# Routing gates of a product-key expert layer: one 256-column fp32r product per token in place of an fp32 product, spread over the projection tile

## The chip, the cores and the metric

The kernel runs on one core of a Trainium2 chip. The core has five engines that run their own instruction streams and meet through semaphores: TensorE (PE, matrix products, with its weight loads shown apart as PEld), VectorE (DVE), ScalarE (ACT), GpSimd (POOL) and SyncE (SP, which issues the transfers here). The metric is the device time of one execution in microseconds (us); lower is better.

## The reference, cut to what matters

The program is one decoder layer over 576 tokens (512 of a prompt, 8 sequences of 8): a normalisation, an input projection, an RWKV-7 branch and a retention branch, their merge and an output projection, and then a layer of 128 x 128 = 16384 single-neuron experts of which each token uses 8 heads x 16. The part that matters here is the last one:

```python
q = (xb @ peer_wq).reshape(PEER_BLOCK, PEER_HEADS, 2, PEER_QDIM // 2)
s = jnp.einsum('bhpd,hpnd->bhpn', q, peer_keys).astype(F32)
sv, si = lax.top_k(s, PEER_TOPK)
cand = sv[:, :, 0, :, None] + sv[:, :, 1, None, :]
sc, flat = lax.top_k(cand.reshape(PEER_BLOCK, PEER_HEADS, PEER_TOPK * PEER_TOPK), PEER_TOPK)
i1 = jnp.take_along_axis(si[:, :, 0], flat // PEER_TOPK, axis=-1)
i2 = jnp.take_along_axis(si[:, :, 1], flat % PEER_TOPK, axis=-1)
e = i1 * N_KEYS + i2
gate = jax.nn.softmax(sc, axis=-1)
h = jax.nn.gelu(jnp.einsum('bhkd,bd->bhk', peer_u[e], xb).astype(F32), approximate=False)
return jnp.einsum('bhk,bhkd->bd', (gate * h).astype(xb.dtype), peer_v[e])
```

The kernel does not gather experts. It computes the hidden value of every expert for every token (all of `peer_u` against all tokens), and weighs it with a gate matrix that is zero wherever a token did not choose the expert.

## The kernel before

Everything stays in fp32 or in fp32r, a form of fp32 that TensorE reads in one pass at lower precision. A product that needs more precision is written as three fp32r products of high and low parts (high x high, high x low, low x high); the high part is a ScalarE copy into fp32r, the low part a VectorE subtraction (`low`, line 140).

**The stage around the change** is `gates_stage`. Its backbone is 128 tiles of the hidden projection, one for each 128 experts. A tile t is 96 matmuls (16 blocks c of the model width; for each, two halves of 288 tokens with three products), written out by `project3` (lines 125, 126, 129) into PSUM buffer t % 2. `segments` gives every engine the same order: 4 x 5 tiles with the `early` steps (the choice of experts for 5 groups of 128 tokens), 4 x 12 tiles with the `middle` steps (the gate matrices), then the rest. An argument `late=1` puts PE, ACT and SP one tile ahead of DVE's count.

The **steps of a tile**, engine by engine:

- PE waits for `lowered` (the low part of the tile's weights) and for `gelu` (the PSUM buffer is free), and runs the 96 matmuls; the last one signals `through` (the semaphore `ah_tile_done`).
- ACT waits for `through`, applies Gelu from PSUM into `hs` (line 1944), waits for the weights of tile t + 2 and casts them into their high part `uh` (line 1947).
- DVE waits for that cast and subtracts into `ul` (line 140), which releases `lowered`.
- SP stores `hs` (line 1887) and loads the next weights, 1 MB (line 1885).

The **middle steps** build, for each token, a 128 x 128 gate matrix: a product of two one-hot blocks summed over the token's 128 choices, where one side carries the gates. Twelve tokens are done per tile, in three groups g of four, so 48 tiles cover 576 tokens:

- DVE: waits for `gated` of the group's last use, writes both one-hot blocks `hot` of four tokens (line 2048).
- POOL: multiplies one of them with the gates into `rows` (line 1974) and signals `rowed`.
- PE: after the tile, and for each group, waits for `rowed` and for `moved` (its PSUM bank is free again), and multiplies `hot` by `rows`, four fp32 matmuls of 128 columns (line 1920), then signals `gated`. There are three PSUM banks, one per group, and ACT starts `moved` at 3, so a group waits only for the same group of the tile before.
- ACT: after Gelu and cast, waits for `gated` and copies the group from PSUM into `stage`, with a stride of 48 elements (line 1963), and signals `moved`.
- SP: after every fourth tile waits for all of `moved` and stores `stage`, 3 MB, to memory (line 1892). ACT's next copy but one round waits for that store.

Afterwards `experts_stage` multiplies the hidden values by the gates and by `peer_v`.

## Time and profile before

| what | us |
|---|---|
| median of 3 runs | 6522.78 (6519.88 to 6525.54) |
| the profiled execution | 6519.62 |
| its span | 6517.8 |
| tiles with middle steps, 48 of them, from about 3282 to about 4020 in the span | about 738 |
| mean granted TensorE clock | 0.979 |

How to read it: the profile shows the span of one execution, 1.8 us less than that execution's time. Each engine's busy time is the union of its instructions. A matmul's duration includes its way through the array, so a stream of them overlaps, and what one costs is the distance between starts. In 40 slices of 163 us PE stands at nine tenths or more in all but a handful, and the slices of the 48 middle tiles are among the fullest.

### The profile page before, as it was taken

The numbers are of one execution on the slowest core, as the hardware profiler recorded it, in microseconds if no ns is written. First come the engines' busy times: TensorE is split into PE (matmuls) and PEld (weight loads), VectorE is DVE, ScalarE is ACT, GpSimd is POOL, SyncE is SP. The second block draws the span as 40 slices with busy tenths as digits, with TensorE's granted clock in tenths as the row PEclk, the third lists the DMA queues.
The fourth block names the chain that finished last, engine by engine and source line by source line (L and its number), as shares of the span: only waits on it lengthen the run. The fifth ranks groups of instructions, "written<-read, shape, count | busy, mean of one in ns | idle before, by whom it ended". The sixth has DMA issues, their size and how long they took to land. (4 is left out here: it accounts for less than half of the span.)

```text
span 6517.8 us, 109245 instructions
## 1 busy us (share of the span) xinstructions
PE 6224.3 (95%) x46455; PEld 5740.2 (88%) x46455; DVE 2750.5 (42%) x4165; ACT 1586.5 (24%) x1919; POOL 324.1 (5%) x250
## 2 busy tenths in 40 slices
PE   7999989999999899698999999999989999999998
PEld 7787879999999899698999999999978888888886
DVE  4566543223222232256744443111145555555554
ACT  3333322222222221221233333111121122112211
POOL 1010000000000000000023232000000000000000
PEclk9999999999999999899999999999999999999999
DMA  2111022222133323122233433333344444444442
GB/s 92 42 39 53 34 75 94 102 88 100 68 136 119 121 101 115 49 72 105 101 130 127 149 138 134 106 107 107 107 129 127 127 123 125 128 127 122 126 128 98
DMA packets 352490, 679.34 MB, mean 104 GB/s; under 512 B 220800, under 2 KB 227968, under 8 KB 311296
## 3 DMA queue, kind: packets, MB, share of 16 engines
q1 hardware_dynamic: 345200, 656.85, 30.7%
q10 hardware_dynamic: 7056, 19.00, 0.7%
q8 instruction: 192, 3.15, 0.2%
q14 instruction: 42, 0.34, 0.0%
HBM read 562.40 MB, written 113.37 MB: 104 GB/s over the span
## 5 line engine op out<-in xcount | busy, mean ns | idle before, releaser
L125 PE MATMUL ps<-hn_high,ah_uh 128*128 128x288 f32 x4096 | 1147.8, 296 | 23.2 <-DVE ah_ul L140 23.1
L126 PE MATMUL ps<-hn_low,ah_uh 128*128 128x288 f32 x4096 | 1140.5, 294 | 0.0
L2159 PE MATMUL ps<-va_vh,va_h_parts 128*128 128x512 f32 x2560 | 1007.2, 393 | 23.8 <-DVE va_h_parts L140 23.8
L2163 PE MATMUL ps<-va_vl,va_h_parts 128*128 128x512 f32 x2560 | 1015.4, 397 | 0.0
L129 PE MATMUL ps<-hn_high,ah_ul 128*128 128x288 f32 x4096 | 880.7, 296 | 0.0
L2161 PE MATMUL ps<-va_vh,va_h_parts 128*128 128x512 f32 x2048 | 814.4, 398 | 0.0
L125 PEld LDWEIGHTS ps<-hn_high,ah_uh 128*128 128x128 f32 x4096 | 771.1, 188 | 24.5 <-DVE ah_ul L140 23.4
L126 PEld LDWEIGHTS ps<-hn_low,ah_uh 128*128 128x128 f32 x4096 | 769.1, 188 | 0.0
L2231 DVE TENSOR_TENSOR va_y<-va_y,ps 128x512 f32<-128x512 f32 x640 | 440.5, 688 | 772.8 <-PE ps L2163 772.8
L140 DVE TENSOR_TENSOR ah_ul<-ah_u,ah_uh 128x2048 fp32r<-128x2048 f32 x128 | 293.5, 2293 | 1085.4 <-ACT ah_uh L1947 1077.2
L129 PEld LDWEIGHTS ps<-hn_high,ah_ul 128*128 128x128 f32 x4096 | 655.5, 188 | 0.0
L2159 PEld LDWEIGHTS ps<-va_vh,va_h_parts 128*128 128x128 f32 x2560 | 483.9, 189 | 137.3 <-issue 24.0
L2163 PEld LDWEIGHTS ps<-va_vl,va_h_parts 128*128 128x128 f32 x2560 | 482.2, 188 | 114.1
L1094 PE MATMUL ps<-rwkv_hn_high,ret_wh 128*128 128x288 f32 x1664 | 494.5, 312 | 16.1 <-DVE ret_wl L140 16.1
L1095 PE MATMUL ps<-hn_low,ret_wh 128*128 128x288 f32 x1664 | 472.1, 298 | 0.0
L2161 PEld LDWEIGHTS ps<-va_vh,va_h_parts 128*128 128x128 f32 x2048 | 383.7, 187 | 95.2
L2182 ACT CAST va_vh<-va_v 128x1024 fp32r<-128x1024 f32 x256 | 255.5, 1045 | 520.0 <-PE ps L2163 512.0
L1944 ACT ACTIVATE ah_h<-ps 128x576 f32<-128x576 f32 x128 | 83.4, 652 | 1226.4 <-PE ps L129 1226.4
L1098 PE MATMUL ps<-rwkv_hn_high,ret_wl 128*128 128x288 f32 x1664 | 358.1, 297 | 0.0
L1094 PEld LDWEIGHTS ps<-rwkv_hn_high,ret_wh 128*128 128x128 f32 x1664 | 320.4, 193 | 28.9 <-DVE ret_wl L140 16.2
L609 PE MATMUL ps<-rwkv_hn_high,rwkv_wh 128*128 128x288 f32 (+1 forms) x960 | 297.1, 324 | 27.2 <-DVE hn_low L140 27.2
L1095 PEld LDWEIGHTS ps<-hn_low,ret_wh 128*128 128x128 f32 x1664 | 319.6, 192 | 2.1
(376 smaller groups left out, 10174.9 us busy)
## 6 DMA issues: line engine op xcount, KB each, us to landing
ah_u<-peer_u SPq DMA_DIRECT2D x128, 1024.0 KB, 5.0
va_v<-peer_v SPq DMA_DIRECT2D x256, 512.0 KB, 3.6
ret_w<-w_ret SPq DMA_DIRECT2D x48, 1024.0 KB, 4.9
h_kept<-ah_h SPq DMA_DIRECT2D x128, 288.0 KB, 2.1
gates<-ah_stage SPq DMA_DIRECT2D x12, 3072.0 KB, 9.7
va_h<-h_kept SPq DMA_DIRECT2D x128, 288.0 KB, 3.1
va_g<-gates SPq DMA_DIRECT2D x128, 288.0 KB, 3.9
rwkv_w<-w_rkv SPq DMA_DIRECT2D x24, 1024.0 KB, 4.8
```

What stands on the lines that cost most here:

```text
L125: pe.matmul(out[:, h, :], wh[:, c, :], ah[:, c, t], start=(c == 0), stop=False)
L126: pe.matmul(out[:, h, :], wh[:, c, :], al[:, c, t], start=False, stop=False)
L129: last = pe.matmul(out[:, h, :], wl[:, c, :], ah[:, c, t], start=False, stop=(c == k - 1))
L140: return dve.tensor_tensor(out, whole, high.bitcast(F32), ALU.subtract)
L609: pe.matmul(z[:, h, :], w, K.hn_high[:, c, t], start=(c == 0), stop=False)
L1094: pe.matmul(z[:, h, :], w, K.high[:, c, t], start=(c == 0), stop=False)
L1095: pe.matmul(z[:, h, :], w, K.low[:, c, t], start=False, stop=False)
L1098: last = pe.matmul(z[:, h, :], v, K.high[:, c, t], start=False, stop=(c == DC - 1))
L2159: done = pe.matmul(Z[bank], mine, high, start=(j == 0), stop=False)
L2161: pe.matmul(Z[bank], hx[:, s, j, 2 * T - TP + P * m:2 * T - TP + P * m + P], high, start=False, stop=False)
L2163: done = pe.matmul(Z[bank], mine, lows, start=False, stop=(j == R - 1))
L2231: dve.tensor_tensor(part, part, Z[bank], ALU.add).then_inc(added, 1)
```

## The change

Each gate matrix is computed in fp32r. `slots[:, 2]` (the gates) is split into `gate_h`, an fp32r copy that ACT makes beside its copy into `slots`, and `gate_l`, a DVE subtraction made once. POOL now makes two products per group, with the high and with the low part, side by side in `rows` (twice its former size). PE makes one matmul of 256 columns per token in place of one fp32 matmul of 128. A group now fills two PSUM banks (high halves and low halves beside each other), so four banks make two buffers, and group g of tile k uses buffer (k + g) % 2; `moved` starts at 2.

On leaving PSUM the halves are added: ACT copies the high half into `stage` and signals `half` (the semaphore `ah_high_half_staged`), and DVE adds the low half from PSUM onto it in `stage` and signals `moved`. After each add DVE writes the one-hot block for the same group one tile ahead; the first three are written before the middle tiles (`ahead`), which also takes them out of the wait for `gated`.

PE's groups no longer stand behind the tile: they follow blocks c = 4, 9 and 15 of the 16. The tile's matmuls are written out in `tile` for that (lines 1916, 1917, 1920 after the change).

The norm stage only allocates fewer semaphores (three lines, not shown).

```diff
@@ -1829,10 +1829,11 @@
             return nc.alloc_sbuf_tensor_at("ah_" + name, shape, dt, offset=place), place + 4 * int(np.prod(shape[1:]))
 
         stage, room = over("stage", [P, ROWS, TC], room)
-        hot, room = over("hot", [P, 2, TURN, P], room)
-        rows, room = over("rows", [P, TURN, P], room)
+        hot, room = over("hot", [P, 2, TURN, P], room, F32R)
+        rows, room = over("rows", [P, TURN, 2, P], room, F32R)
         sb("rest", [P, (room - nc.sbuf_base) // 4])
         iota = sb("iota", [P, P])
+        gate_h, gate_l = sb("gate_high", [P, NTT * P], F32R), sb("gate_low", [P, NTT * P])
         u, base = over("u", [P, 2, DC, P], K.x1_at)
         ul, base = over("ul", [P, 2, DC, P], base, F32R)
         assert base <= K.x1_at + 4 * DC * T
@@ -1845,12 +1846,16 @@
         consts = sem("consts")
         diff, exped, ided, turned, slotted = sem("diff"), sem("exp"), sem("ids"), sem("turned"), sem("slots")
         hotted, rowed, gated, moved = sem("hot"), sem("rows"), sem("gates"), sem("staged")
+        parted, half = sem("gate_parts"), sem("high_half_staged")
         stored = sem("stage_stored")
         Z = [K.ps[:, 2 * n:2 * n + 2, 0:HT] for n in range(2)]
-        X = [K.ps[:, 4 + n, :] for n in range(3)]
+        X = [K.ps[:, 4 + 2 * n:6 + 2 * n, :].rearrange("p b (t x i) -> p b t x i", t=2, x=2) for n in range(2)]
         block = ctx.enter_context(nc.Block())
 
-        def segments(eng, tile, early, middle, late=1):
+        def staged(k, g):
+            return stage[:, :, 12 * k + 4 * g:12 * k + 4 * g + 4].rearrange("p i (b t) -> p b t i", b=2)
+
+        def segments(eng, tile, early, middle, late=1, between=None):
 
             if late:
                 tile(0, 0, True)
@@ -1858,10 +1863,15 @@
                 for k in range(4):
                     tile(4 * i + k + late, (k + late) % 2, True)
                     early(i, k)
+            if between:
+                between()
             with eng.Fori(0, NST) as s:
                 for k in range(4):
-                    tile(EARLY + 4 * s + k + late, (k + late) % 2, True)
-                    middle(s, k)
+                    if eng is nc.tensor:
+                        tile(EARLY + 4 * s + k + late, (k + late) % 2, True, lambda g: middle(s, k, g))
+                    else:
+                        tile(EARLY + 4 * s + k + late, (k + late) % 2, True)
+                        middle(s, k)
             n = (ROWS - 2 - MIDDLE - late) // 2
             with eng.Fori(0, n) as i:
                 for k in range(2):
@@ -1888,7 +1898,7 @@
 
             def middle(s, k):
                 if k == 3:
-                    sp.wait_ge(moved, 12 * s + 15)
+                    sp.wait_ge(moved, 12 * s + 14)
                     sp.dma_start(K.gates[:, s, :, :], stage[:, :, :]).then_inc(stored, 16)
             segments(sp, tile, nothing, middle)
             for s in range(2):
@@ -1897,10 +1907,21 @@
 
         @block.tensor
         def _(pe):
-            def tile(t, s, more):
+            def tile(t, s, more, group=None):
                 pe.wait_ge(lowered, t + 1)
                 pe.wait_ge(gelu, t + 1)
-                project3(pe, Z[s], uh[:, s, :, :], ul[:, s, :, :], K.hh, K.hl).then_inc(through, 1)
+                for c in range(DC):
+                    for h in range(2):
+                        m = slice(h * HT, h * HT + HT)
+                        pe.matmul(Z[s][:, h, :], uh[:, s, c, :], K.hh[:, c, m], start=(c == 0), stop=False)
+                        pe.matmul(Z[s][:, h, :], uh[:, s, c, :], K.hl[:, c, m], start=False, stop=False)
+                    for h in range(2):
+                        m = slice(h * HT, h * HT + HT)
+                        last = pe.matmul(Z[s][:, h, :], ul[:, s, c, :], K.hh[:, c, m], start=False, stop=(c == DC - 1))
+                    if c == DC - 1:
+                        last.then_inc(through, 1)
+                    if group and c in (4, 9, 15):
+                        group((4, 9, 15).index(c))
 
             def early(i, k):
                 if k == 3:
@@ -1911,15 +1932,15 @@
                                             K.ident[:, :])
                     last.then_inc(turned, 1)
 
-            def middle(s, k):
-                for g in range(3):
-                    n = 12 * s + 3 * k + g
-                    pe.wait_ge(rowed, n + 1)
-                    pe.wait_ge(moved, n + 1)
-                    for t in range(4):
-                        last = pe.matmul(X[g][:, P * t:P * t + P], hot[:, 1, 4 * g + t, :], rows[:, 4 * g + t, :],
-                                         start=True, stop=True)
-                    last.then_inc(gated, 1)
+            def middle(s, k, g):
+                n = 12 * s + 3 * k + g
+                pe.wait_ge(rowed, n + 1)
+                pe.wait_ge(moved, n + 1)
+                for t in range(4):
+                    last = pe.matmul(K.ps[:, 4 + 2 * ((k + g) % 2) + t // 2, 2 * P * (t % 2):2 * P * (t % 2) + 2 * P],
+                                     hot[:, 1, 4 * g + t, :], rows[:, 4 * g + t, :, :].rearrange("p x i -> p (x i)"),
+                                     start=True, stop=True)
+                last.then_inc(gated, 1)
             pe.sem_inc(gated, 3)
             segments(pe, tile, early, middle)
 
@@ -1927,7 +1948,7 @@
         def _(act):
             act.sem_inc(gelu, 2)
             act.sem_inc(slotted, 1)
-            act.sem_inc(moved, 3)
+            act.sem_inc(moved, 2)
             act.sem_inc(stored, 16)
             for s in range(2):
                 act.sem_inc(kept[s], 16)
@@ -1952,6 +1973,7 @@
                     act.activation(ids[:, 2, :, :], ids[:, 2, :, :], ACT.Exp).then_inc(exped, 1)
                 if k == 3:
                     act.wait_ge(turned, i + 1)
+                    act.copy(gate_h[:, bass.ds(P * i, P)], K.ps[:, 7, 2 * P:3 * P])
                     act.copy(slots[:, :, bass.ds(P * i, P)], K.ps[:, 7, 0:3 * P].rearrange("p (s t) -> p s t", s=3))\
                         .then_inc(slotted, 1)
 
@@ -1960,19 +1982,21 @@
                     act.wait_ge(stored, 16 * s + 16)
                 for g in range(3):
                     act.wait_ge(gated, 12 * s + 3 * k + g + 4)
-                    act.copy(stage[:, :, 12 * k + 4 * g:12 * k + 4 * g + 4].rearrange("p i t -> p t i"),
-                             X[g].rearrange("p (t i) -> p t i", t=4)).then_inc(moved, 1)
+                    act.copy(staged(k, g), X[(k + g) % 2][:, :, :, 0, :]).then_inc(half, 1)
             segments(act, tile, early, middle)
 
         @block.gpsimd
         def _(pool):
+            pool.wait_ge(parted, 1)
             with pool.Fori(0, NST) as s:
                 for k in range(4):
                     for g in range(3):
                         t = slice(4 * g, 4 * g + 4)
                         pool.wait_ge(hotted, 12 * s + 3 * k + g + 1)
-                        pool.tensor_tensor(rows[:, t, :], hot[:, 0, t, :],
-                                           slots[:, 2, bass.ds(TC * s + 12 * k + 4 * g, 4)]
+                        own = bass.ds(TC * s + 12 * k + 4 * g, 4)
+                        pool.tensor_tensor(rows[:, t, 0, :], hot[:, 0, t, :].bitcast(F32), gate_h[:, own].bitcast(F32)
+                                           .unsqueeze(2).broadcast_to([P, 4, P]), ALU.mult)
+                        pool.tensor_tensor(rows[:, t, 1, :], hot[:, 0, t, :].bitcast(F32), gate_l[:, own]
                                            .unsqueeze(2).broadcast_to([P, 4, P]), ALU.mult).then_inc(rowed, 1)
 
         @block.vector
@@ -2039,16 +2063,24 @@
                         .then_inc(ided, 1)
                     dve.drain()
 
+            def one_hot(g, first):
+                dve.tensor_tensor(hot[:, :, 4 * g:4 * g + 4, :],
+                                  iota[:, :].unsqueeze(1).unsqueeze(1).broadcast_to([P, 2, 4, P]),
+                                  slots[:, 0:2, bass.ds(first, 4)].unsqueeze(3).broadcast_to([P, 2, 4, P]), ALU.is_equal)\
+                    .then_inc(hotted, 1)
+
+            def ahead():
+                dve.wait_ge(slotted, NTT + 1)
+                dve.tensor_tensor(gate_l[:, :], slots[:, 2, :], gate_h[:, :].bitcast(F32), ALU.subtract).then_inc(parted, 1)
+                for g in range(3):
+                    one_hot(g, 4 * g)
+
             def middle(s, k):
-                if k == 0:
-                    dve.wait_ge(slotted, NTT + 1)
                 for g in range(3):
-                    t = slice(4 * g, 4 * g + 4)
-                    dve.wait_ge(gated, 12 * s + 3 * k + g + 1)
-                    dve.tensor_tensor(hot[:, :, t, :], iota[:, :].unsqueeze(1).unsqueeze(1).broadcast_to([P, 2, 4, P]),
-                                      slots[:, 0:2, bass.ds(TC * s + 12 * k + 4 * g, 4)].unsqueeze(3)
-                                      .broadcast_to([P, 2, 4, P]), ALU.is_equal).then_inc(hotted, 1)
-            segments(dve, tile, early, middle, 0)
+                    dve.wait_ge(half, 12 * s + 3 * k + g + 1)
+                    dve.tensor_tensor(staged(k, g), staged(k, g), X[(k + g) % 2][:, :, :, 1, :], ALU.add).then_inc(moved, 1)
+                    one_hot(g, TC * s + 12 * k + 4 * g + 12)
+            segments(dve, tile, early, middle, 0, ahead)
 
 
 def experts_stage(nc, K, a, x1):
```

**PE, from the end of a middle tile to the start of the next one, before.** The names are those of the program; `ps` is PSUM, and a row's waits stand in brackets.

```order
L129 MATMUL ps<-hn_high,ah_ul 128x288 x2
L1917 ISA
L1920 MATMUL ps<-ah_rows,ah_hot 128x128 [waits ah_staged,ah_rows]
L1920 MATMUL ps<-ah_rows,ah_hot 128x128 x3
L1917 REGISTER_ALU
L1920 MATMUL ps<-ah_rows,ah_hot 128x128 [waits ah_staged,ah_rows]
L1920 MATMUL ps<-ah_rows,ah_hot 128x128 x3
L1917 REGISTER_ALU
L1920 MATMUL ps<-ah_rows,ah_hot 128x128 [waits ah_staged,ah_rows]
L1920 MATMUL ps<-ah_rows,ah_hot 128x128 x3
L1901 REGISTER_ALU
L125 MATMUL ps<-hn_high,ah_uh 128x288 [waits ah_gelu_done,ah_u_low]
```

The same place after the change; the first row is among the last three matmuls of block c = 15.

```order
L1917 MATMUL ps<-hn_low,ah_uh 128x288
L1920 MATMUL ps<-hn_high,ah_ul 128x288 x2
L1937 REGISTER_ALU
L1940 MATMUL ps<-ah_rows,ah_hot 128x256 [waits ah_staged,ah_rows]
L1940 MATMUL ps<-ah_rows,ah_hot 128x256 x3
L1911 REGISTER_ALU
L1916 MATMUL ps<-hn_high,ah_uh 128x288 [waits ah_gelu_done,ah_u_low]
```

Three groups of 128 columns have become one group, the third, of 256 columns behind the tile's last matmul, which signals `ah_tile_done`; the other two stand inside the tile, each with the same two waits.

**ACT, one middle tile from its wait for the end of the tile to the first group's copy, before.**

```order
L1943 ISA [waits ah_tile_done]
L1944 ACTIVATE ah_h<-ps 128x576 [waits ah_h_stored0]
L1946 REGISTER_ALU
L1947 CAST ah_uh<-ah_u 128x2048 [waits ah_u_in0]
L1962 REGISTER_ALU
L1963 COPY ah_stage<-ps 128x4x128 [waits ah_gates]
L1962 REGISTER_ALU
```

And after:

```order
L1964 ISA [waits ah_tile_done]
L1965 ACTIVATE ah_h<-ps 128x576 [waits ah_h_stored0]
L1967 REGISTER_ALU
L1968 CAST ah_uh<-ah_u 128x2048 [waits ah_u_in0]
L1984 REGISTER_ALU
L1985 COPY ah_stage<-ps 128x4x128 [waits ah_gates]
L1984 REGISTER_ALU
```

Nothing moved here: the three copies follow the wait for the tile's end, the Gelu and the cast.

**DVE, one middle tile, before** (the low part of the weights, then the one-hot blocks):

```order
L1987 REGISTER_ALU
L140 TENSOR_TENSOR ah_ul<-ah_u,ah_uh 128x2048 [waits ah_u_high]
L2047 REGISTER_ALU
L2048 ISA [waits ah_gates]
L2048 TENSOR_TENSOR ah_hot<-ah_iota,slots 128x2x512
L2047 REGISTER_ALU
L2048 ISA [waits ah_gates]
```

And after:

```order
L140 TENSOR_TENSOR ah_ul<-ah_u,ah_uh 128x2048 [waits ah_u_high]
L2080 ISA
L2081 TENSOR_TENSOR ah_stage<-ah_stage,ps 128x4x128 [waits ah_high_half_staged]
L2067 ISA
L2067 TENSOR_TENSOR ah_hot<-ah_iota,slots 128x2x512
L2080 REGISTER_ALU
L2081 TENSOR_TENSOR ah_stage<-ah_stage,ps 128x4x128 [waits ah_high_half_staged]
L2067 ISA
L2067 TENSOR_TENSOR ah_hot<-ah_iota,slots 128x2x512
L2080 REGISTER_ALU
```

An add that waits for ACT's copy now stands before each one-hot block, and the block is the next tile's.

## Rows read from the trace of the kernel before

**Rows 1.** The page: busy time of each engine, share of the span, instructions.

```profile
PE 6224.3 (95%) x46455; PEld 5740.2 (88%) x46455; DVE 2750.5 (42%) x4165; ACT 1586.5 (24%) x1919; POOL 324.1 (5%) x250
```

**Rows 2.** Busy time by window: early tiles, and middle tiles; first row names columns.

```profile
core 0: us, PE busy (x) PEld busy (x) DVE busy (x) ACT busy (x) POOL busy (x), PEclk, DMA share, GB/s
3080.00:3285.00 205.00, 204.23 (x1535) 202.46 (x1534) 164.49 (x328) 51.46 (x47) 0.00 (x0) 1.00 0.30 103
3290.00:4026.00 736.00, 736.00 (x5746) 736.00 (x5745) 311.65 (x190) 260.77 (x240) 230.83 (x144) 1.00 0.37 134
```

**Rows 3.** PE in order of time: start, duration, instruction, count. Two gate bursts.

```profile
3310.30 2.84 PE L1920 MATMUL ps<-ah_rows,ah_hot 128*128 128x128 f32 x24
3312.90 0.38 PE L125 MATMUL ps<-hn_high,ah_uh 128*128 128x288 f32 x1
...
3325.68 2.84 PE L1920 MATMUL ps<-ah_rows,ah_hot 128*128 128x128 f32 x24
```

**Rows 4.** PE by window: 288-column matmuls only, then 512-column ones (window, length, busy, clock).

```profile
4100.00:4600.00 500.00, 500.00 (x3784) 1.00 0.30 107
5400.00:6300.00 900.00, 900.00 (x3865) 1.00 0.45 126
```

**Rows 5.** PE, then ACT, in order of time around one tile's end; idle before in brackets.

```profile
3617.83 2.84 PE L1920 MATMUL ps<-ah_rows,ah_hot 128*128 128x128 f32 x24
...
3605.12 1.91 ACT L1947 CAST ah_uh<-ah_u 128x2048 fp32r<-128x2048 f32 x1 [1.72 <-DMA ah_u<-peer_u]
...
3618.12 0.65 ACT L1944 ACTIVATE ah_h<-ps 128x576 f32<-128x576 f32 x1 [8.12 <-PE ps L129]
3618.66 1.89 ACT L1947 CAST ah_uh<-ah_u 128x2048 fp32r<-128x2048 f32 x1
3620.45 3.07 ACT L1963 COPY ah_stage<-ps 128x512 f32<-128x512 f32 x3
```

**Rows 6.** Instructions of single lines: durations in ns, minimum, median, maximum.

```profile
L1963 ACT COPY ah_stage<-ps x144: 1102/1197/1238, 3297.6 to 4022.1; 128x512 f32<-128x512 f32 x144
...
L2231 DVE TENSOR_TENSOR va_y<-va_y,ps x640: 686/689/690, 4798.7 to 6466.0; 128x512 f32<-128x512 f32 x160
...
L894 DVE TENSOR_REDUCE rwkv_kk<-rwkv_cs x16: 1059/1064/1085, 211.9 to 918.4; 128x64 f32<-128x512 f32 x16
```

**Rows 7.** PE by window after idle time: first and last of nine, and one between.

```profile
946.97:956.97 10.00, 10.00 (x58) 10.00 (x59) 2.29 (x1) 0.16 (x1) 0.00 (x0) 0.75 0.77 316
...
2677.17:2681.51 4.34, 0.00 (x1) 0.00 (x0) 0.76 (x1) 0.73 (x2) 0.00 (x0) 0.72 0.04 4
2681.51:2691.51 10.00, 9.99 (x32) 7.57 (x33) 0.00 (x0) 9.83 (x16) 0.00 (x0) 0.78 0.01 2
...
6480.44:6490.44 10.00, 10.00 (x34) 7.62 (x35) 0.00 (x0) 9.82 (x16) 0.00 (x0) 0.83 0.00 0
```

**Rows 8.** PE's waits (total, times, longest); then windows behind two such waits.

```profile
PE ps L657 <- DVE rwkv_ksq L805: 17.9, 7, 2.6
...
339.83:346.83 7.00, 6.69 (x34) 6.26 (x34) 6.40 (x10) 1.92 (x2) 0.00 (x0) 0.76 0.26 101
...
239.40:246.40 7.00, 5.15 (x34) 4.71 (x34) 6.40 (x10) 1.91 (x2) 0.00 (x0) 1.00 0.27 110
```

**Rows 9.** VectorE and GpSimd instructions of the middle steps, durations in ns as in group 6.

```profile
L2048 DVE TENSOR_TENSOR ah_hot<-ah_iota,slots x144: 1215/1221/2066, 3287.5 to 4009.4; 128x1024 f32<-128x1024 f32 x144
...
L1974 POOL TENSOR_TENSOR ah_rows<-ah_hot,slots x144: 1033/1857/2021, 3288.9 to 4012.3; 128x512 f32<-128x512 f32 x144
```

**Rows 10.** VectorE in order of time, one middle tile: weights' low part, one-hot blocks.

```profile
3620.59 2.29 DVE L140 TENSOR_TENSOR ah_ul<-ah_u,ah_uh 128x2048 fp32r<-128x2048 f32 x1 [6.99 <-ACT ah_uh L1947]
3622.80 4.33 DVE L2048 TENSOR_TENSOR ah_hot<-ah_iota,slots 128x1024 f32<-128x1024 f32 x3
```

**Rows 11.** SyncE's queue: the store of the stage and the next load of weights.

```profile
3592.93 0.33 SPq L1892 DMA_DIRECT2D gates<-ah_stage  x1
3593.80 0.35 SPq L1885 DMA_DIRECT2D ah_u<-peer_u  x1
```

**Rows 12.** ScalarE's copies into the slots, durations in ns, first and last start.

```profile
L1955 ACT COPY slots<-ps x5: 473/482/483, 3078.2 to 3285.2; 128x384 f32 x5
```

More of the change, by code:

```diff
@@ L146, in norm_stage @@
     with ExitStack() as ctx:
-        ld = [ctx.enter_context(nc.semaphore(tag + f"_loaded{q}")) for q in range(4)]
+        ld = [ctx.enter_context(nc.semaphore(tag + f"_loaded{q}")) for q in range(4)] if load is not None else []
         sq = ctx.enter_context(nc.semaphore(tag + "_squared"))
@@ L152, in norm_stage @@
         dn = ctx.enter_context(nc.semaphore(tag + "_normed"))
-        st = ctx.enter_context(nc.semaphore(tag + "_stored"))
-        hi = ctx.enter_context(nc.semaphore(tag + "_high"))
+        st = ctx.enter_context(nc.semaphore(tag + "_stored")) if store is not None else None
+        hi = ctx.enter_context(nc.semaphore(tag + "_high")) if parts else None
         rstd = ctx.enter_context(nc.sbuf_tensor(tag + "_r", [P, T], F32))
```

## The prediction

> **What bounds the kernel now.** I read the page first: TensorE is busy 95% of the span [rows 1]. That is an average, so I went to the windows of the gates stage. In the 736 us that hold nearly all the middle tiles PE is busy for all 736 us at full granted clock; DVE is busy 312 us, ACT 261, POOL 231 [rows 2]. So here every microsecond of PE work counts in full, and everything else has more than half its time free. Then PE in order of time, for what one middle tile consists of. From one gate burst to the next it is 3325.68 - 3310.30 = 15.38 us. The burst, 24 records for 12 tokens, holds PE from 3310.30 to 3312.90, which is 2.60 us [rows 3]. A plain 288-column matmul costs 500 / 3784 = 0.132 us [rows 4], so 96 of them are 12.68 us, and the burst's whole price is 15.38 - 12.68 = 2.70 us.
>
> **What the change removes.** The 24 records (two per fp32 product) become 12 matmuls of 256 columns. Rows show 0.132 us for 288 columns and 900 / 3865 = 0.233 us for 512 [rows 4]; on the line through both, 256 columns cost 0.118 us, 12 of them 1.41 us. So PE's own work falls by 2.70 - 1.41 = 1.29 us per tile, 62 us over 48 tiles. If the clock and the waits stay as they are, that is the whole effect.
>
> The page "FP8 and Floating Point Precision" of the Trainium skill (TensorE Precision Notes) has true fp32 take four passes through the array, which would put the new product at half of the old one's columns, 1.35 us per tile and a saving of 65 us. The trace shows two records per product, not four, and I keep the line through its two rows.
>
> **What the change adds: a wait behind the tile.** Follow the third group, g = 2. It uses the same PSUM buffer as g = 0 of the same tile, (k + g) % 2. `moved` starts at 2, and group n waits for n + 1, so it needs n - 1 groups moved, the last of which is g = 0 of its own tile. That group was multiplied early, after block 4. But who moves it? ACT's copy stands in ACT's queue behind the wait for the end of the same tile, the Gelu and the cast; the order of ACT's instructions is unchanged. So PE finishes its 96 matmuls, arrives at g = 2 and stands still until ACT has worked down to g = 0 and DVE has added the low half. Before, with three banks, a group waited for the group of the tile before, long done.
>
> The length of this stand, from the moment PE would issue g = 2:
>
> 1. to the Gelu's start: 3618.12 - 3617.83 = 0.29 us [rows 5].
> 2. Gelu to the start of the cast 0.54 us, cast to the start of the first copy 1.79 us [rows 5].
> 3. the first copy to its end: 1.10 us, the lowest of its line, since the first of three is the shortest [rows 6]. Sum so far 3.72 us. The copy of the high half has the same 512 elements and the same stride of 48, so I keep its price.
> 4. DVE's add, 512 elements from PSUM and strided `stage` back to `stage`. No row shows it. The same add without a stride takes 0.69 us (L2231); a reduction that reads 512 elements with a stride of 64 takes 1.06 us (L894) [rows 6]. ACT's strided copy takes 1.20 us. I take 1.06, the nearest in kind, with bounds of 0.69 and 1.5 (both read and write strided). DVE is idle at this time.
> 5. two hand-overs between engines, about 0.1 us together.
>
> That is 3.72 + 1.06 + 0.1 = 4.9 us per tile, in full on PE, since PE's queue is in order and the next tile's first matmul stands behind g = 2. The period becomes 12.68 + 1.41 + 4.9 = 19.0 us against 15.38: +3.6 us per tile, 48 tiles, +174 us.
>
> **The clock.** PE never stands still in the middle tiles now; then it would for nearly 5 us in each. In the trace of before there are, past its first 100 us, nine stands of 3 us or more, and behind each the granted clock is at its lower level, 1.2 GHz, for part of the next 10 us: the mean of the nine is 0.77, from 0.72 to 0.83, the stand of 4.34 us has 0.78 [rows 7]. Behind stands of 2.3 to 2.6 us it is mixed: 0.76 in one 7 us window, 1.00 in another [rows 8]. So 4.9 us should always cost clock. A mean of 0.78 over 10 us is 2.2 us of full-speed work lost; bounds 1.7 and 2.8. I take 2.2 us per tile, +106 us. Nothing hides it, since PE is the chain. The period is then 21.2 us.
>
> **Smaller parts.**
>
> - First middle tile: the first one-hot blocks wait for `slots`. ACT's last copy starts at 3285.2 [rows 12] and gets a small copy ahead of it (0.2 us); DVE's subtraction of 640 elements (0.75 us by L140's 2.29 us for 2048) and a one-hot block of 1.22 us follow, then two POOL products of 1.0 to 2.0 us. `rowed` comes at about 3290 to 3292, while PE is at block 4 at about 3286. One stand of some 5 us with 2 us of clock: +7 us, once.
> - POOL: two products where there was one. Alone one takes 1.03 us, beside DVE's one-hot block up to 2.02 [rows 9]. Six are 6.2 to 12.1 us in a period of 21 us. For the next tile's g = 0: its one-hot block starts when the add ends at 4.9, ends at 6.1, and two products are done at 8.2, or 9.4 if DVE's next block goes between. PE wants them five blocks after g = 2, at 4.9 + 0.5 + 4.0 = 9.4 us, and 2 us later at the low clock. No wait.
> - DVE: weights' low part 2.29, three blocks 4.33 [rows 10], three adds 3.2, together 9.8 us; the low part is late in the period, at about 15 us, but it is wanted one tile later. Hidden. The subtraction of the whole `gate_l` is in the first part.
> - SP: the store waits for the last add, about 9.4 us behind the tile's end in place of 5.9, and the load of weights behind it (3593.80 after 3592.93 [rows 11]) is as late. Today the cast behind such a store waits 1.72 us for that load [rows 5], and PE doesn't notice. With a period of 21.2 us, 5.8 longer, the 3.5 us of delay are covered: 0. With a period of 19.0 they are nearly not: up to 1.7 us for each of 11 stores.
>
> **Sum.** Period: 21.2 - 15.38 = 5.8 us x 48 = 280 us, plus 7 = 287 us. On the profiled execution's 6519.6 us that gives 6807; the median of the runs is 3.2 us higher, so 6810 us. The gain of 62 us is in this sum; it is paid back four times over.
>
> **Rivals.**
>
> - *The clock stays up.* For it: one 2.58 us stand left it at 1.00 [rows 8], and PE is dense around the stand. Against: all nine stands over 3 us lowered it. Then 48 x 3.6 + 5 + 11 x 1.7 = 197 us: 6720 us; with the cheap add of 0.69 us 6700.
> - *More waits than the one.* If the add costs 1.5 us and POOL's products reach g = 0 about 1 us late, each tile is 1.4 us longer: 6877. Rows 9 show that a one-hot block of 1.22 us becomes 2.06 us beside POOL, and POOL's product doubles. The Trainium skill, "SBUF — State Buffer" (Who interferes with whom), calls this an exclusive lock: a DVE instruction with two SBUF inputs and a GpSimd one that reads SBUF take turns whole. By it POOL's two products wait for at most one block between them, the 9.4 us above. The add reads one operand from PSUM and would be free of it.
> - *Faster.* The mechanism is the shorter burst alone: g = 2 finds its buffer free, because group 0 is moved before the tile ends. It decides at one point, the place of ACT's first copy: it would have to be ahead of ACT's wait for the tile's end. Then -62 us and +7: 6519.6 - 55 + 3.2 = 6468. Against it stands the order of ACT's instructions, where it is behind. Only a misreading of the semaphore's count could save this case.
> - *No change*, where a short stand of about 1.2 us without clock loss cancels the gain: 6523. No row gives such a length.
>
> **Chances.** Forecast 0.75 (its own range, from the bounds of add and clock: 6765 to 6860), clock stays up 0.10, more waits 0.08, faster 0.05, same 0.02. The range of 6700 to 6890 takes in the first three. A difference under 0.2%, 13 us, couldn't be told from no change here; by that, faster 0.05, same 0.02, slower 0.93.
>
> **What the profile of the changed kernel would show.** In the middle tiles, PE no longer busy throughout: about 4.9 us idle in each of 48 tiles, ended by DVE's add into `ah_stage`; Gelu starts 19 to 21 us apart; 12 products per tile at 0.118 us where the clock is full; a granted clock of about 0.8 to 0.9 as the mean of the stretch. The add between 0.7 and 1.5 us. The tiles before and after the middle unchanged at 12.7 us, and the stages around them too. What would make it wrong: idle time of PE ended by POOL's `rows` in every tile (the second rival), a clock of 1.00 (the first), or no idle time before g = 2 (the third).

## The result, and the profile after

| | us |
|---|---|
| before, median (4 runs) | 6521.77 (6519.88 to 6525.54) |
| changed, median (4 runs) | 6782.63 (6780.55 to 6786.51) |
| changed / before | 1.040, 95% interval 1.039 to 1.041 |
| profiled execution, before and changed | 6519.62 and 6780.63 |
| 48 tiles, from the Gelu of the first middle tile to the Gelu behind the last one, before and changed | 738.1 and 991.0 |

The change costs 4%. The page's first lines, as in rows 1:

```profile
PE 6251.6 (92%) x45879; PEld 5758.1 (85%) x45879; DVE 2944.9 (43%) x4313; ACT 1581.6 (23%) x1924; POOL 574.4 (8%) x394
```

DVE and POOL have 194 and 250 us more to do, PE much the same over a longer span. The windows of the gates stage answer to rows 2: the early tiles, the middle tiles, and plain tiles behind them (columns as there).

```profile
3080.00:3285.00 205.00, 204.20 (x1535) 202.46 (x1534) 164.56 (x328) 51.84 (x50) 0.00 (x0) 1.00 0.29 103
3290.00:4276.00 986.00, 761.32 (x5150) 751.48 (x5150) 498.04 (x331) 250.11 (x236) 480.24 (x287) 0.90 0.27 99
4330.00:4770.00 440.00, 440.00 (x3329) 440.00 (x3329) 80.24 (x35) 85.45 (x70) 0.00 (x0) 1.00 0.31 106
```

Before and behind the middle tiles nothing moved: early tiles have the same busy time to 0.1 us on PE. In the middle tiles PE, which was busy all the time, is idle for 225 of 986 us, at a granted clock of 0.90. I call such idle time of PE before an instruction a stand. The list of waits in the stage says who ends it (who waits, for whom, total, times, longest; not all rows are shown):

```profile
PEld ps L1940 <- issue: 237.0, 48, 5.3
PE ps L1940 <- DVE ah_stage L2081: 227.1, 48, 5.1
ACT ah_stage L1985 <- PE ps L1940: 76.2, 48, 1.7
...
PEld ps L1940 <- POOL ah_rows L1999: 5.8, 1, 5.8
PE ps L1940 <- POOL ah_rows L1999: 5.6, 1, 5.6
```

48 waits, one in each middle tile, 4.73 us on average, all before a gate product and all ended by DVE's add. One more, 5.6 us, is the first tile's. Here is one of the 48 in order of time, PE, ACT and DVE (start, duration, instruction, idle time before it); it answers to rows 5.

```profile
3613.03 0.43 PE L1920 MATMUL ps<-hn_high,ah_ul 128*128 128x288 f32 x2
3618.23 1.19 PE L1940 MATMUL ps<-ah_rows,ah_hot 128*128 128x256 f32 x4 [4.78 <-DVE ah_stage L2081]
...
3613.57 0.65 ACT L1965 ACTIVATE ah_h<-ps 128x576 f32<-128x576 f32 x1 [13.60 <-PE ps L1920]
3614.12 1.89 ACT L1968 CAST ah_uh<-ah_u 128x2048 fp32r<-128x2048 f32 x1
3615.91 1.87 ACT L1985 COPY ah_stage<-ps 128x512 f32<-128x512 f32 x2
3619.46 1.06 ACT L1985 COPY ah_stage<-ps 128x512 f32<-128x512 f32 x1 [1.68 <-PE ps L1940]
...
3616.95 1.13 DVE L2081 TENSOR_TENSOR ah_stage<-ah_stage,ps 128x512 f32<-128x512 f32 x1 [10.01 <-ACT ah_stage L1985]
```

Read from top to bottom in time it is the chain of the prediction: the tile's last matmuls at 3613.03, Gelu at 3613.57, cast, the copy of group 0 at 3615.91, the add at 3616.95, and 0.15 us after the add's end PE goes on with group 2 at 3618.23. Its four products take 1.19 us with their way through the array, at the lower clock; four such products take 0.64 us at full clock elsewhere in the tile.

Durations of single lines in ns, minimum, median and maximum: the new product, and the add.

```profile
L1940 PE MATMUL ps<-ah_rows,ah_hot x576: 277/283/583, 3292.0 to 4281.2; 128*128 128x256 f32 x192
...
L2081 DVE TENSOR_TENSOR ah_stage<-ah_stage,ps x144: 1008/1127/1261, 3307.7 to 4283.4; 128x512 f32<-128x512 f32 x144
```

The median distance between two of these products' starts is 0.118 us at full clock.

### The profile page after: what moved, and what is told of

The parts are those of the page before. It is cut to its first block and busy times, and to the rows that moved or that the text cites. A ratio compares the mean times of both kernels' runs of the same rounds, so it can differ in the third digit from the quotient of the medians.

```text
span 6778.9 us, 108539 instructions
## 1 busy us (share of the span) xinstructions
PE 6251.6 (92%) x45879; PEld 5758.1 (85%) x45879; DVE 2944.9 (43%) x4313; ACT 1581.6 (23%) x1924; POOL 574.4 (8%) x394
## 5 line engine op out<-in xcount | busy, mean ns | idle before, releaser
L1916 PE MATMUL ps<-hn_high,ah_uh 128*128 128x288 f32 x4096 | 1178.3, 302 | 23.0 <-DVE ah_ul L140 22.9
L1917 PE MATMUL ps<-hn_low,ah_uh 128*128 128x288 f32 x4096 | 1172.1, 300 | 0.0
L1920 PE MATMUL ps<-hn_high,ah_ul 128*128 128x288 f32 x4096 | 896.4, 301 | 0.0
L1916 PEld LDWEIGHTS ps<-hn_high,ah_uh 128*128 128x128 f32 x4096 | 802.0, 196 | 24.3 <-DVE ah_ul L140 23.1
L1917 PEld LDWEIGHTS ps<-hn_low,ah_uh 128*128 128x128 f32 x4096 | 798.8, 195 | 0.0
L1920 PEld LDWEIGHTS ps<-hn_high,ah_ul 128*128 128x128 f32 x4096 | 673.7, 193 | 0.0
L140 DVE TENSOR_TENSOR ah_ul<-ah_u,ah_uh 128x2048 fp32r<-128x2048 f32 x128 | 333.5, 2606 | 657.3 <-ACT ah_uh L1968 649.3
L2081 DVE TENSOR_TENSOR ah_stage<-ah_stage,ps 128x512 f32<-128x512 f32 x144 | 161.6, 1122 | 491.2 <-ACT ah_stage L1985 491.2
L1997 POOL TENSOR_TENSOR ah_rows<-ah_hot,ah_gate_high 128x512 fp32r<-128x512 f32 x144 | 248.6, 1726 | 1062.3 <-DVE ah_hot L2067 1062.3
```

The lines of the kernel that those rows point to most:

```text
L140: return dve.tensor_tensor(out, whole, high.bitcast(F32), ALU.subtract)
L1916: pe.matmul(Z[s][:, h, :], uh[:, s, c, :], K.hh[:, c, m], start=(c == 0), stop=False)
L1917: pe.matmul(Z[s][:, h, :], uh[:, s, c, :], K.hl[:, c, m], start=False, stop=False)
L1920: last = pe.matmul(Z[s][:, h, :], ul[:, s, c, :], K.hh[:, c, m], start=False, stop=(c == DC - 1))
```

## Experiments: what makes PE stand

My theory (A) was that group 2 waits for a buffer that ACT can only empty after the end of the same tile. The rivals were that the stand has a length of its own (the add, the new products), and that spreading the groups over the tile costs by itself. All ratios are to the kernel before on the same chip. Each edit is shown in part; the label of the run stands in its heading, and the text calls it by its first part (e1, e2 and so on).

### Group 0 and 1 copied before the tile's end (`e1_early_copy`)

```diff
+                    elif eng is nc.scalar:
+                        middle(s, k, (0, 1))
+                        tile(EARLY + 4 * s + k + late, (k + late) % 2, True)
+                        middle(s, k, (2,))
```

The last argument names the groups that ACT copies there.

> The changed kernel, but ACT copies groups 0 and 1 of a tile before it waits for that tile's end; only group 2 is copied after Gelu and cast. Theory A (the stand before group 2 is ACT's queue order): three of four tiles take 12.68 + 1.41 = 14.1 us with no stand. The tile behind each store still stands: the copy of its group 0 waits until the stage is in memory (store issued about 5.5 us after the tile's end, 9.7 us to land, then 1.1 of copy and 1.1 of add: about 17.4 us, where PE wants group 2 at 14.1), 3 us of stand and up to 1.7 us of clock in 11 tiles. Time about 6520 - 62 + 8 + 11 x 4.5 = 6515 us (6480 to 6530). Rival B (the stand is the length of the add or the group products themselves, wherever the copy stands): 20.6 us per tile as in the changed kernel, 6780 us.

Measured: 6517.85 us, ratio 0.999 (0.998 to 1.000). The stands are gone in all but the tiles behind a store (PE's waits in this kernel's stage):

```profile
PE ps L1944 <- DVE ah_stage L2085: 30.4, 11, 2.8
```

and those come from ACT's copy waiting for the store of the stage:

```profile
ACT ah_stage L1989 <- DMA gates<-ah_stage: 122.1, 11, 11.1
```

Most rounds of four tiles take 14.1, 14.2, 16.2 and 16.6 us from Gelu to Gelu: ACT's late copy delays the Gelu behind it, so that one stand of 2.8 us and the clock behind it show in two of them. In nine of the eleven rounds the clock fell; in the other two the last of the four takes 15.1 us. Theory A holds: moving two copies in one queue, with the add, the products and the spread as they were, takes back 265 us. Of the gain of 62 us about 6 are left, at the edge of the noise, since a copy early in the tile meets a store that takes 9.6 us to land.

### The same, with the stage stored in two halves (`e2_early_copy_half_stage`)

```diff
-        stage, room = over("stage", [P, ROWS, TC], room)
+        stage, room = over("stage", [P, 2, ROWS, TC // 2], room)
...
-                if k == 3:
-                    sp.wait_ge(moved, 12 * s + 14)
-                    sp.dma_start(K.gates[:, s, :, :], stage[:, :, :]).then_inc(stored, 16)
+                if k % 2:
+                    sp.wait_ge(moved, 12 * s + 3 * k + 5)
+                    sp.dma_start(K.gates[:, 2 * s + k // 2, :, :], stage[:, k // 2, :, :]).then_inc(stored[k // 2], 16)
```

> As e1_early_copy, and the stage is stored in two halves of 24 tokens, each by its own transfer after every second tile, so no copy waits for a store (in memory the gates lie in runs of 96 bytes instead of 192, which the experts stage reads). Theory A: all middle tiles take 14.1 us but the first, clock 1.00, 6520 - 62 + 8 = 6466 us (6455 to 6480), faster than both kernels. Rival B: 6780 us. Rival C (shorter runs make the reads of the gates late in the experts stage): the middle tiles as in A, but the experts stage longer by some of its 128 reads, over 6480 us.

Measured: 6472.88 us, ratio 0.992 (0.990 to 0.994), faster than both kernels. A stretch of 600 us of its middle tiles has PE without a gap at full clock:

```profile
3300.00:3900.00 600.00, 600.00 (x4575) 600.00 (x4575) 464.86 (x296) 280.69 (x211) 339.29 (x255) 1.00 0.41 148
```

48 tiles take 678.4 us, 14.13 each, which is 59.7 us less than before. The first middle tile's stand costs 9.0 us of that again. The reads of the gates in the experts stage take a median of 4.5 us instead of 3.9, and that stage is no longer for it (1671.8 us against 1671.3 from its first to its last such matmul in the changed kernel): rival C falls.

### Two plain tiles ahead of the middle ones (`e7_two_plain_tiles`)

```diff
-    EARLY = 4 * NTT
+    EARLY = 4 * NTT + 2
...
+            for t in range(4 * NTT, EARLY):
+                tile(t + late, (t + late) % 2, True)
```

> e2_early_copy_half_stage with two plain tiles between the early and the middle ones, so that the split of the gates and the first one-hot blocks have a tile's time before PE wants them. Theory A (the rest of the loss is one stand of 5.8 us in the first middle tile and the clock behind it, 9.0 us from one Gelu to the next): 6473 - 9 = 6464 us (6458 to 6470). Rival G (PE's wait moves with the middle tiles, since a later step sets it): 6473 us.

Measured: 6470.06 us (6464.6 to 6471.3), ratio 0.992 (0.990 to 0.993). In the profile the first stand is gone and the stage is 8.3 us shorter than in e2, from its first Gelu to its last; the medians differ by 2.8 us, within the spread of either. The mechanism is shown, its worth in the time is not resolved.

### The spread alone, first attempt (`e5_spread_only`)

```diff
-                project3(pe, Z[s], uh[:, s, :, :], ul[:, s, :, :], K.hh, K.hl).then_inc(through, 1)
...
+                    if group and c in (4, 9, 15):
+                        group((4, 9, 15).index(c))
```

> The kernel before with one part of the change alone: its fp32 products of 128 columns, three single PSUM banks and ACT's copies stay, but the three groups follow blocks 4, 9 and 15 of the tile instead of standing behind it. Theory A (the spread does no harm by itself; the stand comes from two buffers for three groups): each group still waits only for the same group of the tile before, so no stand, 15.4 us per tile, time within 0.2% of the kernel before (6510 to 6535 us), a few us up for the first tile, whose group 0 waits for its one-hot block. Rival E (breaking up the tile costs: each of three entries and exits of a burst has its own gap): 0.1 to 0.2 us per entry, 5 to 20 us slower.

Measured: 6764.54 us, ratio 1.037 (1.036 to 1.039). My expectation was wrong, and so was that of rival E. PE's waits:

```profile
PE ps L1933 <- POOL ah_rows L1987: 149.9, 46, 4.5
```

PE stands 3.3 us before group 0, for POOL. In the kernel before, the one-hot blocks of a tile are written after the low part of the weights, at the beginning of the tile, and PE wanted them 12.7 us (96 x 0.132) after the tile's first matmul. Behind block 4 it wants them after 4.0 us (30 x 0.132). So this run said nothing about the spread itself; it showed that the spread needs the lookahead on DVE that the change also brings.

### The spread with its lookahead, and then two banks instead of three (`e9_spread_ahead`, `e10_two_banks`)

The first adds the change's `ahead` and one-hot blocks a tile early to e5; the second differs from it in the banks and the counts that go with them.

```diff
-                    last = pe.matmul(X[g][:, P * t:P * t + P], hot[:, 1, 4 * g + t, :], rows[:, 4 * g + t, :],
+                    last = pe.matmul(X[(k + g) % 2][:, P * t:P * t + P], hot[:, 1, 4 * g + t, :], rows[:, 4 * g + t, :],
...
-            act.sem_inc(moved, 3)
+            act.sem_inc(moved, 2)
```

> e5_spread_only (fp32 products, three single banks, groups behind blocks 4, 9 and 15) with the change's other half of the order: DVE writes the one-hot block of a group one tile ahead. In e5 PE stood 3.2 us before group 0, waiting for POOL's product of that tile's own one-hot block. Theory A (that wait is the missing lookahead, and with three banks nothing else stands): 15.4 us per tile, clock 1.00, 6522 + 9 for the first tile = 6531 us (6525 to 6545). Rival E (breaking the tile up costs by itself): over 6545 us, or PE idle inside the tiles.

> e9_spread_ahead with one thing changed: two PSUM banks instead of three, group g in bank (k + g) % 2, as in the changed kernel. No fp32r, no halves, no add. Theory A (the count of buffers with ACT's queue order is the whole cause): PE stands before group 2 from the tile's end to the end of ACT's first copy, 0.3 + 0.5 + 1.8 + 1.1 = 3.7 us, plus 1.6 us of clock: 20.7 us per tile, about 6785 us (6770 to 6800). Rival I (the add on DVE or the fp32r form is part of the cause): as e9, 6531 us.

Measured: 6538.60 us, ratio 1.002 (1.001 to 1.003), and 6789.26 us, ratio 1.041 (1.039 to 1.043). PE's waits, the first kernel's and then the second's:

```profile
PE ps L1935 <- ACT ah_stage L1978: 6.4, 11, 0.7
```

```profile
PE ps L1935 <- ACT ah_stage L1978: 161.8, 45, 3.6
```

With three banks the spread costs 14 us: 6 us in the first middle tile, and 0.8 us in every fourth, where ACT waits for the weights behind the store and is late with a bank. With two banks each tile takes 20.8 us, 3.6 of them a stand, here ended by ACT's copy since there is no add. This is the cleanest evidence for the cause: fp32 products of 128 columns, no halves, no add, and all of the loss, from a buffer count and a queue's order.

## Experiments: the price of the products

One run, `e6_one_pass_128`, on the kernel before:

```diff
-        hot, room = over("hot", [P, 2, TURN, P], room)
-        rows, room = over("rows", [P, TURN, P], room)
+        hot, room = over("hot", [P, 2, TURN, P], room, F32R)
+        rows, room = over("rows", [P, TURN, P], room, F32R)
```

> The kernel before with its twelve products per tile in fp32r and 128 columns, the high part alone (the low part of the gates is left out of the computation), groups behind the tile as before. Theory A (an fp32r product costs by its columns, on the line of 0.118 us for 256 and 0.132 for 288): 0.06 us each, 0.73 us per tile in place of 2.70, time 6522 - 48 x 1.97 = 6427 us. Rival F (a short product is bounded by its weight load, as the two passes of the fp32 one with 0.111 us per 128 columns may be): up to 0.11 us each, 1.3 us per tile, 6455 us; then the second 128 columns of the change cost next to nothing on PE.

Measured: 6457.82 us, ratio 0.990 (0.989 to 0.992). This kernel leaves out the low part of the gates. Its tiles take 14.04 us, and the median distance between two products is 0.111 us, within 0.001 us the distance between the two records of an fp32 product. So rival F has the price right: 128 columns in fp32r cost 0.111 us, as much as one of the two records in fp32, and 256 columns cost 0.118. The line through 288 and 512 columns was good down to 256 and fails at 128, where it gives 0.060. That the weight load sets this price was not shown. The low half of the change costs PE 0.007 us per token; almost all of its gain comes from one record in place of two.

## Experiments: the clock behind the stand

### The stand filled with work (`e3_filler`)

```diff
                     if c == DC - 1:
                         last.then_inc(through, 1)
+                        if group:
+                            pe.wait_ge(gelu, t + 2)
+                            for x in range(36):
+                                pe.matmul(K.ps[:, 2 * (1 - s):2 * (1 - s) + 2, 0:HT][:, x % 2, :], K.hh[:, c, 0:P],
+                                          K.hh[:, c, 0:HT], start=True, stop=True)
```

`pe.wait_ge(gelu, t + 2)` asks for the Gelu of the tile before, which is long done: the extra matmuls start at once.

> The changed kernel with 36 more 288-column matmuls per middle tile, between the tile's end and group 2, into the PSUM buffer that the next tile overwrites; they are no part of the result and take 36 x 0.132 = 4.75 us, the length of the stand. Theory A (4.7 us of stand, and 1.6 us per tile from the lower clock behind it): PE is never idle for more than 0.3 us, the clock stays at 1.00, the period falls from 20.65 to about 19.0 us although PE does more work, time 6780 - 48 x 1.6 = 6703 us (6690 to 6715). Rival D (the 1.6 us are waits inside the tile or slower group products, not clock): the period stays at 20.6 or grows, 6780 us or more.

Measured: 6736.09 us, ratio 1.032 (1.031 to 1.034). PE does 36 matmuls more per tile and the kernel is 47 us faster than the changed one: the clock was a part of the loss (first the changed kernel's stretch, then this one's, then who waits in it).

```profile
3300.00:3900.00 600.00, 462.56 (x3125) 456.63 (x3124) 304.87 (x203) 154.26 (x145) 291.38 (x174) 0.90 0.28 102
```

```profile
3300.00:3900.00 600.00, 586.21 (x4402) 579.68 (x4402) 317.82 (x211) 165.32 (x152) 305.58 (x184) 1.00 0.28 104
```

```profile
PE ps L1945 <- DVE ah_stage L2086: 19.4, 22, 1.7
ACT ah_uh L1973 <- DMA ah_u<-peer_u: 20.3, 12, 4.7
```

It is 33 us slower than I expected. Two parts of that show in its trace: ACT's cast waits 1.4 us for the weights behind each store (eleven times; the wait of 4.7 us comes behind the last middle tile), which is now on the chain (every fourth tile takes 20.6 to 20.8 us instead of 19.2 to 19.5), and copy and add are nearly 0.1 us longer each, so that group 2 starts 5.05 us behind the tile in the median instead of 4.86. In the eleven tiles behind a store 1.5 to 1.7 us of idle time are left, and the clock fell in none of them.

### The stand shortened (`e4_copy_before_gelu`)

```diff
             def tile(t, s, more, first=None):
                 act.wait_ge(through, t + 1)
+                if first:
+                    first()
                 act.wait_ge(kept[s], turns16(t, s))
```

where `first` is the copy of group 0.

> The changed kernel, but ACT copies group 0 right after the tile's end, before Gelu and cast. Theory A (the stand is a chain whose links add up): Gelu 0.54 and cast 1.79 us leave the chain, so the stand falls from 4.7 to about 2.4 us; clock as behind the 2.3 to 2.6 us stands of the kernel before, lost in some tiles only, 0 to 1.7 us per tile. Period 14.1 + 2.5 + 0 to 1.7 = 16.6 to 18.3 us, time 6590 to 6670 us. Rival B (the stand has a fixed length set by add or product): 6780 us.

Measured: 6625.77 us, ratio 1.015 (1.013 to 1.017). PE's waits:

```profile
PE ps L1943 <- DVE ah_stage L2086: 121.9, 48, 3.2
```

The stand is 2.5 us on average: Gelu and cast left the chain, and its links add up. Tiles take 16.8 us, which is 14.1 + 2.6, or 18.3, with 1.5 us of clock. Where group 0's copy waits for a store, the Gelu behind it is 0.8 us late (a tile of 17.6 us) and the stand is 3.0 to 3.2 us; four such stands took more of the clock (19.4 us). By these lengths the clock fell in 13 of 48 tiles: in 8 of the 38 with a stand of 2.4 or 2.5 us, and in 5 of the 10 with one of 3.0 to 3.2. The mean clock of the stretch is 0.96:

```profile
3300.00:3900.00 600.00, 512.92 (x3706) 505.33 (x3705) 334.70 (x238) 177.77 (x170) 310.99 (x206) 0.96 0.32 118
```

### Half of the filling, three quarters of it (`e8_half_filler`, `e11_filler_27`)

> The changed kernel with 18 extra matmuls behind the tile in place of e3_filler's 36 (no part of the result): the wait ends at the same time, but PE idles about 2.5 us of it. Theory A (the clock falls by how long PE idles, not by the wait): loss between none and the full 1.6 us per tile, as in e4_copy_before_gelu (18.3 us where the clock fell, 16.8 where not), period 19.3 to 20.2, time 6740 to 6775 us. Rival H (any wait of PE on VectorE costs the same clock): 20.65 us, 6780 us.

> The changed kernel with 27 extra matmuls behind the tile (no part of the result), so that PE idles about 1.2 us of the wait. With 36 the clock stayed at 1.00, with 18 (2.4 us idle) it fell in nearly every tile. If the clock needs a longer idle time than 1.2 us to fall: period 19.2 to 19.5, as with 36, 6736 us. If any idle time does it: 20.6, 6783 us.

Measured: with 18 matmuls 6783.56 us, ratio 1.040 (1.039 to 1.042); with 27, 6734.74 us, ratio 1.033 (1.031 to 1.035). PE's waits in the one with 18 and in the one with 27, then the stretch of each:

```profile
PE ps L1945 <- DVE ah_stage L2086: 106.8, 45, 2.7
```

```profile
PE ps L1945 <- DVE ah_stage L2086: 73.4, 47, 2.8
```

```profile
3300.00:3900.00 600.00, 530.97 (x3656) 524.91 (x3655) 303.99 (x203) 153.85 (x145) 290.59 (x176) 0.91 0.28 102
```

```profile
3300.00:3900.00 600.00, 552.46 (x4109) 545.47 (x4107) 316.28 (x211) 166.00 (x154) 301.45 (x180) 0.99 0.29 106
```

With 18 the stand is 2.4 us, half of the changed kernel's, and the whole price is paid, in 45 of 48 tiles by their length. That is over the range I gave: it is the time that rival H named, and what speaks against H is e3, e4 and e11. In e11 the mean of 1.6 us is made of two lengths: 37 stands of 1.1 to 1.3 us, none of which cost the clock, and 11 of 2.6 to 2.8 us behind the stores, of which three did. So short stands are free of it, and the price at 2.4 us did not fit e4, where stands of that length cost the clock in 8 of 38 tiles.

### The same idle time in a longer tile (`e12_longer_tile`)

```diff
+                    if group and c == 12:
+                        pe.wait_ge(gelu, t + 2)
+                        for x in range(17):
+                            pe.matmul(K.ps[:, 2 * (1 - s):2 * (1 - s) + 2, 0:HT][:, x % 2, :], K.hh[:, c, 0:P],
+                                      K.hh[:, c, 0:HT], start=True, stop=True)
```

added to e4, so that the stand is left alone and the tile gets longer.

> e4_copy_before_gelu with 17 extra matmuls after block 12 of each middle tile (no part of the result), far from the stand: the stand of 2.5 us stays, the period without clock loss becomes 16.8 + 2.2 = 19.0 us, that of e8_half_filler. Theory J (for the same idle time, the period decides how often the clock falls: e8 with 20.6 us lost it in nearly every tile, e4 with 16.8 in about every third): it falls in nearly every tile here, period about 20.5, 6522 + 48 x 5.1 + 9 = 6776 us. Rival K (what stands beside the idle time decides, not the period): as in e4, a mean loss of 0.7 us, period 19.7, 6738 us.

Measured: 6777.07 us, ratio 1.039 (1.037 to 1.041). Its stretch and PE's waits:

```profile
3300.00:3900.00 600.00, 525.48 (x3631) 519.55 (x3632) 288.66 (x207) 149.99 (x145) 268.98 (x178) 0.91 0.28 103
```

```profile
PE ps L1948 <- DVE ah_stage L2091: 108.7, 45, 2.5
```

All tiles but the first take 20.4 to 20.6 us. The stand is 2.4 us as in most tiles of e4, only the work between two stands is longer, and the clock goes from 0.96 to 0.91. So between these two kernels the distance between stands decides how often a stand of this length costs the clock. It is not the whole rule: in e1, stands of 2.7 to 2.8 us come some 60 us apart and cost it in nine of eleven cases; in e11, stands of 2.6 to 2.8 us with short ones between them did in three of eleven. The five kernels with idle times of 2.4 to 4.7 us (the changed one, e5, e8, e10 and e12) have in common that the granted clock, where it falls in one tile after the other, falls every 20.5 us: in the changed kernel at 3576.9, 3597.4, 3617.9, 3638.4 and 3658.8. Most of their tiles take 20.3 to 20.8 us. Why the two agree, and why at this distance, no run shows; that is open.

## Why the prediction was right, point by point

The forecast was 6810 us, 287 us more than before; measured are 6782.63 us, 261 more. The wait and the clock behind it are both there as forecast, and no other term is large.

- **The bound, and the products.** 12 products of 0.118 us, as worked out, and a period without stand of 14.13 us in e2 against 14.09. Right.
- **The wait behind the tile.** It was read off the order of instructions and the semaphore's start value alone, and it came in each of 48 tiles before group 2, ended by the add. Its length, 4.9 us in the sum, was 4.9 on average from the point where PE would have gone on, from 4.7 to 5.2; the links from Gelu to copy were 0.55 and 1.79 us in most tiles, the copy 1.01 instead of 1.10, the two hand-overs 0.18 instead of 0.1, the add 1.01 to 1.13 where 1.06 was taken from a reduction with a stride. No row had shown the add or the hand-overs, and the copy's error cancels that of the hand-overs: that the sum is right to 0.1 us is in part luck. e1, e2, e4 and e10 each changed the chain and the time followed. Right.
- **The clock.** The mechanism was right, its size was the mis-sized term: 2.2 us per tile, from the 10 us behind the stand of 4.34 us, the nearest in length [rows 7], where 20.65 - 14.13 - 4.9 = 1.6 us was lost. 0.6 us x 48 = 29 us is the whole of the distance between 6810 and 6783. The granted clock behind each stand says much the same: 1.4 to 1.7 us of full-speed work lost in 40 of the 48 tiles, 2.0 to 3.1 in eight. In the tile shown above the clock is at its lower level until 3.1 us after PE goes on; behind the stand of 4.34 us it was so for 4.4 us. The nine stands were a poor sample: seven of them last 15 us or more. The shortest, of 3.1 us, has 0.83 over 10 us, which is 1.7 us and the nearest to what was measured. What makes the clock come back earlier here wasn't tried.
- **The rival in which the clock stays up** (6720 us) is what e3 made: 6736 us. Its 11 or 12 waits of ACT for the weights behind a store, which the forecast held to be covered by the longer period, are in e3, as that rival said, and in the changed kernel they are not: 0.5 us in all.
- **First middle tile.** 7 us expected, 9.0 measured from Gelu to Gelu, of which 0.9 are eight products that the forecast counts in its 48 tiles; a stand of 5.6 us, ended by POOL's product as said.
- **POOL and DVE.** They get in each other's way: POOL's second product takes 2.02 us where DVE's one-hot block stands beside it and 1.04 where none does, and DVE's 2.29 us subtraction 3.12. PE waited for a product of POOL in no tile but the first. By the Trainium skill ("SBUF — State Buffer", Who interferes with whom) a DVE instruction with two SBUF inputs contends with a GpSimd one that reads SBUF, and one with at most one SBUF input does not. The first part agrees with these durations. The add, with one operand in PSUM, took 1.01 us alone and 1.15 beside a product of POOL (medians), 1.26 at most: it was never held up for a whole product.
- **The rule of four passes** ("FP8 and Floating Point Precision", TensorE Precision Notes, of the Trainium skill) has true fp32 take four passes through the array. The estimate from it was 1.35 us per tile for the new products, where 12 x 0.118 = 1.41 was measured. The trace shows two records per fp32 product, 0.111 us each, and e6 shows that one fp32r product of 128 columns costs as much as one record, not a quarter of the fp32 product. Whether each record holds two passes, no run shows.
- **Not in the prediction:** that the spread by itself would have stood before group 0 without the new lookahead on DVE (e5). It changed nothing in the sum, since the change brings both.

## What to carry to other kernels

When the number of buffers falls below the number of groups in flight, follow each wait to the instruction that ends it and look at what stands ahead of that in its own queue: here a copy behind a wait for the very tile whose engine waits for the copy. Such a wait can be priced before a run from the durations of the rows between, and its cure was a few lines in one queue, plus a store in halves so that the earlier copy doesn't meet the transfer. Stands that repeat in a matmul stream can cost more than their length, because the clock comes back late: 1.6 us more for each stand of 4.7 us here, nothing for stands of 1.1 to 1.7 us.

## What the runs showed of the hardware that I had not expected

- A 128-column fp32r product costs 0.111 us (e6), as much as one of the two records of an fp32 product, and a 256-column fp32r product 0.118 us: twice the columns for 6% more time.
- PE idle for 2.4 us, with 18 us from one stand to the next, loses the clock nearly every time (e12: 47 of 48, mean clock 0.91); with the same idle time and 14 us between stands it does in 8 of 38 (e4, 0.96); stands of 1.1 to 1.7 us never did (48 of them in e3 and e11).
- Filling 48 waits of 4.7 us with useless matmuls made the kernel 47 us faster than leaving PE idle (e3).
